# Latent attention of a two-layer encoder on one core: ScalarE moves the turned probabilities of unit i-2 ahead of, not behind, the exponentials of unit i

## What is computed

```
s = einsum('bqhc,bqkc->bqhk', q_lat_b, c_sel)        # scores against the selected latents
s = where(valid, s, -inf)
p = softmax(s, axis=-1)
o_lat = einsum('bqhk,bqkc->bqhc', p, c_sel)          # probabilities times latents
o = einsum('bshc,hcd->bshd', o_lat, w_uv)
```

## Time and profile before

| what | number |
|---|---|
| median of 3 runs | 2592.58 us (2591.0 to 2593.51) |
| the profiled execution | 2587.56 us, span 2585.8 us |
| TensorE busy in the span | 2488.4 us, 96% |
| VectorE, ScalarE, GpSimd busy | 1549.3, 1008.7, 215.1 us |
| granted TensorE clock, mean | 0.983 of full speed |
| the attention stage in the trace | 586 to about 793 us |

### The profile page before, as it was taken

The page is one execution under the profiler, slowest core; times in us unless marked ns, Lnnn a source line. Parts: engine busy times, 40 slices in busy tenths (PEclk is TensorE's granted clock), DMA queues, the critical chain, the costliest instruction groups (busy, mean ns, idle before and its releaser), DMA issues.

```text
span 2585.8 us, 33956 instructions
## 1 busy us (share of the span) xinstructions
PE 2488.4 (96%) x13076; PEld 1955.7 (76%) x13078; DVE 1549.3 (60%) x2649; ACT 1008.7 (39%) x1816; POOL 215.1 (8%) x243
## 2 busy tenths in 40 slices
PE   7999999998898999999999998998999999999998
PEld 5587777875546788888888786776878888888786
DVE  6379976855544685656543546728576566553444
ACT  4323324545433343333332433428444333333333
POOL 4015533410000000000010000000000000000000
PEclk8999989999999999999999999999999999999999
DMA  5121100000003322222364341110332322336342
GB/s 174 48 74 41 41 25 10 3 34 1 1 25 121 131 74 82 83 80 82 90 225 146 133 137 41 43 39 28 96 114 82 98 66 87 94 100 234 122 159 102
DMA packets 207184, 217.54 MB, mean 84 GB/s; under 512 B 12496, under 2 KB 174304, under 8 KB 203568
## 3 DMA queue, kind: packets, MB, share of 16 engines
q1 hardware_dynamic: 204080, 196.13, 24.4%
q0 software_dynamic: 2944, 19.24, 2.1%
HBM read 172.35 MB, written 42.47 MB: 83 GB/s over the span
## 4 chain that ended last, share of the span: by engine, by line
PE 88%; DVE 6%; ACT 4%; issue 2%; POOL 0%; DVEq 0%; ACTq 0%; POOLq 0%
PE ps L333 24%; PE ps L334 24%; PE ps L335 24%; PE ps L2887 2%; PE ps L2864 1%; PE ps L2875 1%; ACT d_p L1524 1%; DVE met L2012 1%; PE ps L2251 1%; PE ps L2265 1%; PE ps L2260 1%; PE ps L1797 1%; PE ps L2304 1%; PE ps L2228 1%; PE ps L2313 1%
## 5 line engine op out<-in xcount | busy, mean ns | idle before, releaser
L322 DVE TENSOR_TENSOR wlo<-wraw,whi 128x1024 fp32r<-128x1024 f32 x152 | 186.4, 1227 | 370.0 <-ACT whi L316 369.6
L316 ACT ACTIVATE whi<-wraw 128x1024 fp32r<-128x1024 f32 x166 | 175.0, 1055 | 354.3 <-PE ps L335 337.6
L333 PE MATMUL ps<-ahi,whi 128*128 128x512 f32 x704 | 275.3, 391 | 6.5 <-DVE hT L960 4.3
L334 PE MATMUL ps<-alo,whi 128*128 128x512 f32 x704 | 273.9, 389 | 0.0
L335 PE MATMUL ps<-ahi,wlo 128*128 128x512 f32 x704 | 273.9, 389 | 0.0
L333 PE MATMUL ps<-uhi,whi 128*128 128x512 f32 x608 | 244.7, 402 | 8.2 <-DVE ulo L492 4.2
L333 PE MATMUL ps<-q_T,whi 128*128 128x512 f32 x640 | 249.2, 389 | 1.6 <-ACT upr L761 1.6
L335 PE MATMUL ps<-q_T,wlo 128*128 128x512 f32 x640 | 249.0, 389 | 0.0
L334 PE MATMUL ps<-q_T,whi 128*128 128x512 f32 x640 | 249.0, 389 | 0.0
L333 PE MATMUL ps<-q_B,whi 128*128 128x512 f32 x608 | 238.9, 393 | 2.4 <-DVE q_B L492 2.4
L335 PE MATMUL ps<-uhi,wlo 128*128 128x512 f32 x608 | 238.0, 392 | 0.0
(11 more groups left out here) (459 smaller groups left out, 4517.8 us busy)
## 6 DMA issues: line engine op xcount, KB each, us to landing
wraw<-in_ffn_w_down_dram SPq DMA_DIRECT2D x88, 512.0 KB, 3.7
wraw<-in_ffn_w_gate_dram SPq DMA_DIRECT2D x44, 512.0 KB, 4.7
araw<-acts SPq DMA_DIRECT2D x88, 256.0 KB, 3.9
wraw<-in_ab_w_in_dram SPq DMA_DIRECT2D x24, 512.0 KB, 3.8
park<-hT POOLq DMA_DIRECT2D x3, 4096.0 KB, 11.5
wraw<-in_ffn_w_up_dram SPq DMA_DIRECT2D x24, 512.0 KB, 5.2
acts<-sgA SPq DMA_DIRECT2D x12, 1024.0 KB, 4.6
raw<-in_ffn_w_up_dram SPq DMA_DIRECT2D x20, 512.0 KB, 4.0
```

The costliest lines, as they stand in the source:

```text
L316: nc.scalar.activation(as_raw(whi[:, t.slot, :]), raw, ACT.Copy).then_inc(S("w_high"), 1)
L322: eng.tensor_tensor(as_raw(wlo[:, t.slot, :]), raw, as_raw(whi[:, t.slot, :]).bitcast(F32), ALU.subtract).then_inc(S("w_split"), 1)
L333: nc.tensor.matmul(dst, wh, xh, start=start, stop=False, **kw)
L334: nc.tensor.matmul(dst, wh, xl, start=False, stop=False, **kw)
```

## The change

Two lines of `att_act` stand ahead of the exponential of the step instead of behind it. No instruction is added or taken out.

```diff
             N = len(AU)
             for i in range(N + 6):
+                if 2 <= i < N + 2:
+                    att_move(act, 0, i - 2, copy)
                 if i < N:
                     b, h = AU[i]
                     act.wait_ge(*after("at_masked", i + 1))
...
                 if i == 0:
                     normed_out(act, NB - 1)
-                if 2 <= i < N + 2:
-                    att_move(act, 0, i - 2, copy)
                 if i >= 6 and i % 4 == 2:
```

## The result

| | time, us | ratio to before (95% interval) |
|---|---|---|
| before | 2593.05 median (2591.0 to 2598.22, 6 runs) | |
| after | 2576.31 median (2573.94 to 2580.89, 6 runs) | 0.9933 (0.9918 to 0.9947) |

What follows compares the result with a forecast made beforehand. TensorE was taken to bound the attention stage, idling for late ScalarE moves. Terms 2.60 + 5.03 + 1.50 + 3.55 + 0.75 = 13.4 us, off the 2592.6 median, gave 2579.2 us, range 2575 to 2587.

Steps and rivals of the forecast that it cites:

- The bound: Latent attention stage: TensorE sets the pace, and its turns wait 19 times, 14.1 us in total, for ScalarE moves.
- (a): Turns 40, 48 and 56, each the last before a `values`: the whole wait for ScalarE goes, 2.60 us.
- the 0.17 added for the lap of a matmul's modelled end: Added to each stated TensorE wait, because a matmul's modelled end laps 0.17 us over the next start.
- (b): Turns 33-36, 41-44, 49-52 (heavy selection pieces on VectorE): VectorE's copy limits the gain, 5.03 us; turns 57-60, without selection: 1.50 us.
- (c): Turns 37, 45, 53, 61, behind the copy of ya: the move comes at once, before the exponential, 3.55 us.
- (d): The stage's end, no scores left: turn 63 can start near 779.1 instead of 780.81; 0.75 us counted here.
- Blocks 0 to 3: One group per unit, only even units ScalarE's: 0 gain taken, with ends of minus 6.7 and plus 0.4 us.
- Passing through: Output projection behind the stage, TensorE busy 104.8 of 105 us: the stage's gain passes through whole.
- Nothing gained: Rival: VectorE's copy or the masking is right behind ScalarE's wait everywhere, time stays 2592.6 us; chance 0.07.
- a half: Rival: VectorE's chain or a lengthened PSUM copy takes most of the select-stretch gain and part of that behind ya, 2584.0 us; chance 0.15.
- slower: Rival: a move at the head of ScalarE's in-order queue delays exponentials in blocks 0 to 3, 6.7 us, 2599.3; chance 0.05.
- All waits going: Rival: every wait goes if VectorE's chain moves forward as well, 16.6 us, 2576.0 us; chance 0.05.

## Why the prediction was right

**The bound.** TensorE sets the pace and its idle time is what can be won: the halves of the change show it. In blocks 4 to 7 the stage got shorter by 13.75 us of the 16.6 that its waits had cost; most of the rest is in the waits that are left, 1.6 us for VectorE's copies and 1.0 for ScalarE's moves. In block 1, where a later wait took over, nothing came of it.

**(a), turns 40, 48, 56**: forecast 2.60. The kernel with the old order behind `ya` has it by itself. In its trace the three turns start 0.87, 0.86 and 0.87 us sooner behind their scores than before (1.29, 1.51 and 1.71 us instead of 2.16, 2.37 and 2.58), 2.60 together, so the waits go whole and the 0.17 added for the lap of a matmul's modelled end holds in the narrower blocks too. The stretches gain a little more, 1.03 + 0.96 + 0.88 = 2.87 us. The largest part of the difference is turn 39: it started 1.47 us behind its scores and now starts 1.34 behind them, without a wait in the list of before. I had no term for this.

**(b), the select stretches and 57 to 60**: forecast 5.03 + 1.50, measured 5.13 + 1.54. The step that mattered, to take the stretch's gain from the end of VectorE's copy and not from the sum of ScalarE's waits, is shown by the halt within turn 52 and by the kernel that pulls that copy forward. The premise that VectorE's chain would not move holds as well: the copy of unit 51 starts 15.11 us behind the `values` of turn 48 before (726.21 and 711.10) and after (719.27 and 704.16).

**(c), behind `ya`**: forecast 3.55, measured 3.16 (0.81, 0.91, 0.97 and 0.47). It was too high only in the last, where 0.85 became 0.47: without this part of the change turn 61 comes late, but turn 62 then waits less.

**(d), the end**: forecast 0.75, measured 1.05 (15.97 to 14.92 with the old order behind `ya`). Together (c) and (d) of the last stretch are 1.52 against 1.60, so the split between the two was off and the sum was not. Exponential 63 kept its place as said: it starts right behind its masking and 3.26 us behind scores 63 (762.01), where it was 3.19. But turn 63 comes 2.01 us behind it, not 1.85, since turn 62 and the `outs` behind it now lie between:

```profile
764.79 0.61 ACT L2944 ACTIVATE PT<-ps 128x512 f32<-128x512 f32 x1
765.08 0.08 DVE L2983 DVE_READ_ACCUMULATOR2_ANT nmx<- 128x1 f32 x1
...
765.27 1.17 ACT L2953 ACTIVATE sm<-sm,nmx 128x1024 f32<-128x1024 f32 x1
...
765.54 1.06 PE L2875 MATMUL ps<-unit,acc 128*128 128x128 f32 x8 [0.78 <-ACT PT L2944]
...
767.28 1.04 PE L2875 MATMUL ps<-unit,sm 128*128 128x128 f32 x8
```

**Blocks 0 to 3**: forecast 0, measured 0 (5.73 to 5.75, 7.87 to 7.88, and so on). **Passing through**: no loss behind the stage is seen, within the scatter of the rest, which takes 1789.1 to 1793.6 us over the traces.

**The rivals.** Nothing gained, a half (8.6 us, 0.9967) and slower are out by the interval. (Against the slower one the prediction set 33.4 us of ScalarE's waits for masking; that was the `sm` buffers alone, and with `acc` it was 50.8.) The mechanism of the slower one does exist, ScalarE waits 22 times for a turn, but the turn always came while the masking was still running; one unit closer it begins to cost, 2.4 us and not tens. All waits going (16.6 us, 2576.0) can't be told from the forecast by the first six runs, whose median of 2576.31 even lies nearer to it. It is out by the traces: the stage is 13.75 us shorter, and the three waits for VectorE that took over stand in the list. The rule of the Trainium skill (Perfetto Trace Analysis, Identifying the Most-Contended Engine) would have had a sum of 0 here, if it is read as an order to leave the emptier engines alone. Its own follow-up, to see what ends the gaps of the fullest engine, gave the 13.4; the measurement decides for that reading.

**The total.** 2579.2 was forecast and 2576.31 measured, inside the range. The 3 us between them are not in the stage; the two repeats put the median at 2579.06 and 2575.67, on chips where the kernel before took 2590.78 and 2591.63. The right size of the stage's gain is no luck, since it holds term by term; how much of the 15.5 us of the three ratios lies outside the stage is open.

## What to carry to other kernels

In a hand-ordered software pipeline, ask of every copy that frees a buffer whether it stands behind work whose input comes from the engine it blocks. If its own input has long been there (here ScalarE waited for it ahead of only 2 of 48 moves), try it in front. That is no rule for every engine: the same edit on VectorE won 0.2 us a stretch in a few places and lost 1.3 at the end. Price the gain by what is next in line, here the end of the other engine's copy, and not by the sum of the waits; and look at the last iterations apart, where nothing fills in. Then look at that next one: 0.9 us of VectorE's work, moved behind the copy that TensorE waited for, made the stage another 4.9 us shorter.

## What the runs showed of the hardware

The same instructions with the same waits ahead of them found the clock at full or at half at the stage's end in different executions (granted 1.00 in two traces, and in two others 0.52 over 4 us and 0.72 over 6 us). The last stretch and the way to the projection are 4.5 us longer in the first of the two slowed traces and 1.7 us in the second. The Trainium skill (TensorE: Matmul & The Clock Gate, Part 1) says that activity releases TensorE's clock and that it drops back otherwise; the traces agree with that, since TensorE was busy only about 2.0 of the 4 us ahead of turn 62. They show besides that the same idleness does not always bring it about: it was 2.03 us where the clock fell and 1.96 where it stayed at full.

A stage can be read from the distances of one marker instruction. Where the clock was the same, each of the eight distances repeated to 0.01 us in the three traces of the changed kernel and in the two of the kernel before, although the spans of the latter differ by 2.7 us. That told apart effects of 0.2 us which no timing of the whole kernel could.
